# First modulation vectors by columns, squares summed on TensorE tile by tile

## What is computed

```python
m_lat = split(silu(c) @ w_mod[0] + b_mod[0], 6)          # shift, scale, gate, ...
h_lat = rmsnorm(x, g_pre_mix[0]) * (1 + m_lat[1]) + m_lat[0]
m_ctx = split(silu(c_ctx) @ w_mod[0] + b_mod[0], 6)
h_ctx = rmsnorm(ctx, g_pre_mix[0]) * (1 + m_ctx[1]) + m_ctx[0]
d = h_lat @ w_dqkv                                      # the first large product
```

## Time and profile before

| | |
|---|---|
| time of three runs | 2483.79 us median (2473.08 to 2486.47) |
| the profiled execution's own time | 2476.99 us |
| its span in the trace | 2474.6 us |
| PE busy | 2414.3 us, 98% |
| PEld busy | 1955.1 us, 79% |
| DVE busy | 1844.6 us, 75% |
| ACT busy | 1209.1 us, 49% |
| POOL busy | 612.5 us, 25% |
| granted TensorE clock, mean | 0.987 of full speed |

### The profile page before, as it was taken

The page is one execution under the profiler, slowest core; times in us unless marked ns, Lnnn a source line. Parts: engine busy times, 40 slices in busy tenths (PEclk is TensorE's granted clock), DMA queues, the critical chain, the costliest instruction groups (busy, mean ns, idle before and its releaser), DMA issues.

```text
span 2474.6 us, 32113 instructions
## 1 busy us (share of the span) xinstructions
PE 2414.3 (98%) x11124; PEld 1955.1 (79%) x11124; DVE 1844.6 (75%) x2786; ACT 1209.1 (49%) x1948; POOL 612.5 (25%) x473
## 2 busy tenths in 40 slices
PE   7989999999899999999999999999999999999998
PEld 3878888888788788888888787766887888888886
DVE  5467676767637988888655879998579888887556
ACT  3356565666643544544454542244645544445542
POOL 0058586874033300010000321100432001010002
PEclk9999998999999999999999999999999999999999
DMA  6046465652432455555865567711314555558655
GB/s 271 27 145 175 124 174 160 187 144 68 136 124 78 120 146 140 141 132 139 247 221 187 179 196 183 157 39 47 115 56 128 146 144 132 134 139 265 211 183 178
DMA packets 153203, 366.31 MB, mean 148 GB/s; under 512 B 14432, under 2 KB 15712, under 8 KB 153056
## 3 DMA queue, kind: packets, MB, share of 16 engines
q1 hardware_dynamic: 107056, 242.69, 28.4%
q0 software_dynamic: 44416, 116.93, 21.9%
q10 hardware_dynamic: 1584, 4.85, 0.6%
HBM read 303.07 MB, written 136.31 MB: 178 GB/s over the span
## 4 chain that ended last, share of the span: by engine, by line
PE 71%; DVE 18%; POOL 4%; DMA 3%; issue 3%; ACT 1%; SPq 0%; DVEq 0%; POOLq 0%; ACTq 0%
PE psum L2305 21%; PE psum L2307 21%; PE psum L2306 21%; DVE acts L2215 3%; DVE acts L2217 3%; PE psum L2521 2%; DMA set<-mod_w 1%; POOL set L837 1%; DVE weights_f32r L1850 1%; PE psum L2510 1%; PE psum L2511 1%; POOL set L836 1%; DVE acts L2219 1%; DMA low<-x_t 1%; POOL low L837 1%
## 5 line engine op out<-in xcount | busy, mean ns | idle before, releaser
L2305 PE MATMUL psum<-acts_f32r,weights_f32r 128*128 128x512 f32 x1536 | 606.4, 395 | 9.3 <-DVE acts_f32r L1610 3.0
L2307 PE MATMUL psum<-acts_f32r,weights_f32r 128*128 128x512 f32 x1536 | 599.1, 390 | 0.0
L2306 PE MATMUL psum<-acts_f32r,weights_f32r 128*128 128x512 f32 x1536 | 598.6, 390 | 0.0
L955 ACT ACTIVATE weights_f32r<-low 128x512 fp32r<-128x512 f32 (+2 forms) x471 | 303.8, 660 | 449.0 <-DVE low L1996 257.4
L2305 PEld LDWEIGHTS psum<-acts_f32r,weights_f32r 128*128 128x128 f32 x1536 | 288.9, 188 | 71.8 <-issue 6.2
L2307 PEld LDWEIGHTS psum<-acts_f32r,weights_f32r 128*128 128x128 f32 x1536 | 288.7, 188 | 61.3
L2306 PEld LDWEIGHTS psum<-acts_f32r,weights_f32r 128*128 128x128 f32 x1536 | 289.1, 188 | 58.7 <-issue 0.5
L862 POOL TENSOR_TENSOR low<-low 128x512 f32<-128x512 f32 x91 | 133.8, 1471 | 691.9 <-ACT low L1194 685.9
L2305 PE MATMUL psum<-high_f32r,weights_f32r 128*128 128x512 f32 (+1 forms) x485 | 192.1, 396 | 0.0
L2307 PE MATMUL psum<-high_f32r,weights_f32r 128*128 128x512 f32 (+1 forms) x485 | 186.9, 385 | 0.0
L2306 PE MATMUL psum<-high_f32r,weights_f32r 128*128 128x512 f32 (+1 forms) x485 | 186.8, 385 | 0.0
(11 more groups left out here) (254 smaller groups left out, 4702.0 us busy)
## 6 DMA issues: line engine op xcount, KB each, us to landing
low<-units SPq DMA_DIRECT2D x130, 512.0 KB, 4.2
set<-mod_w POOLq DMA_DIRECT2D x80, 512.0 KB, 3.9
low<-gated_sums SPq DMA_DIRECT2D x110, 256.0 KB, 4.5
low<-weight_sums SPq DMA_DIRECT2D x88, 256.0 KB, 4.1
gated_sums<-low SPq DMA_DIRECT2D x22, 768.0 KB, 3.5
low<-units SPq DMA_DIRECT2D x66, 256.0 KB, 5.0
weight_sums<-units POOLq DMA_DIRECT2D x14, 1024.0 KB, 10.1
residual<-low SPq DMA_DIRECT2D x48, 256.0 KB, 2.0
```

The source lines that it names most:

```text
L955: return act.activation(out, in_, ACT.Copy, scale=scale)
L2305: pe.matmul(out, wl, xh, start=first, stop=False, skip_group_check=continued)
L2306: pe.matmul(out, wh, xl, start=False, stop=False, skip_group_check=continued)
L2307: return pe.matmul(out, wh, xh, start=False, stop=last, skip_group_check=continued)
```

## The change

The scale and the shift vector of the first layer are made another way round. `mod_vectors` takes a 128x128 block of the weights as the stationary operand and the two columns of silu as the moving one. 8 such matmuls a tile, 64 a vector, give the result in columns at once, in bank 6 (scale) and bank 2 (shift). The copies of rows on ACT and DVE, `ROWS`, the transposes and their semaphores go.

The squares of x aren't added up on DVE any more. PE takes every squared tile as 8 stationary blocks against one column of ones, accumulating in PSUM over the tiles: 64 matmuls for 8. The squares have three buffers, and ACT waits for PE (`sq_used`) before it overwrites one. `spin` is made 16 long for 14 ahead of that, and 8 long behind the shift vector.

On PE the order becomes: scale vector, `spin`, all squares, shift tiles 0 and 1, `spread`, shift tiles 2 to 7, `spin(8, 0)`, `first_two`. On DVE the shift vector is taken up behind the sixth of the 8 `scaled`; the seventh follows it, and the eighth stands behind the third `h_low`.

```diff
-            return f(F_ACC) if n in (0, CB) else f((F_SQ if n < CB else F_LATSQ) + (n + 1) % 2 * L)
+            return f(F_SQ + n % 3 * L) if n < CB else f(F_ACC) if n == CB else f(F_LATSQ + (n + 1) % 2 * L)
...
                 square_full(k, A(k))
-                if k == 3:
-                    act.wait_ge(rows_done, 1)
-                    copy(ROWS[0:2, 0:HALF], PS[0:2, 0:HALF]).then_inc(row_out, 1)
             std(N_A, D, CB, 1)
-            act.wait_ge(rows_done, 2)
-            act.wait_ge(cols_out, 1)
-            copy(ROWS[0:2, 0:HALF], PS[0:2, 0:HALF]).then_inc(row_out, 1)
...
-            for k in range(1, CB):
-                add_square(k)
-                if k == 3:
-                    dve.wait_ge(rows_done, 1)
-                    dve.tensor_copy(ROWS[0:2, HALF:L], PS[0:2, HALF:L]).then_inc(row_out, 1)
-                if k == 5:
-                    dve.wait_ge(cols_out, 1)
-                    mod_columns(1, N_SCALE)
-                    gain(C_AV, V_PREMIX, C_MOD + CB, 1)
-                    gain(C_AX, V_PREMIX, C_MODX + CB, 1)
+            dve.wait_ge(cols_out, 1)
+            mod_columns(1, N_SCALE, 6)
+            gain(C_AV, V_PREMIX, C_MOD + CB, 1)
+            gain(C_AX, V_PREMIX, C_MODX + CB, 1)
             spread(CB, F_ACC)
             rt_here()
-            for k in range(CB):
+            for k in range(CB - 2):
                 scaled(x_block, col(C_AV), RT, k)
-            dve.wait_ge(rows_done, 2)
-            dve.tensor_copy(ROWS[0:2, HALF:L], PS[0:2, HALF:L]).then_inc(row_out, 1)
             dve.wait_ge(mod_mm, 1)
-            mod_columns(0, N_SHIFT)
+            mod_columns(0, N_SHIFT, 2)
             dve.sem_inc(shift_out, 1)
             dve.sem_inc(mod_out, 2)
+            scaled(x_block, col(C_AV), RT, CB - 2)
             for k in range(CB):
                 h_low(x_block, lambda k: h(k, 0), lambda k: h(k, 1), col(C_MOD), k)
+                if k == 2:
+                    scaled(x_block, col(C_AV), RT, CB - 1)
...
+            def mod_vectors(w, at, k, b):
+
+                for c in range(CB):
+                    mm = pe.matmul(bank(b, 2, at + 2 * c), w[:, c * P:(c + 1) * P], S[:, C_SC + 2 * k:C_SC + 2 * k + 2],
+                                   start=k == 0 and c == 0, stop=k == CB - 1 and c == CB - 1)
+                return mm
+
             spin(16, 5)
             for k in range(CB):
-
                 pe.wait_ge(scale_in[k // 2], 16)
-                for half in range(2):
-                    mm = pe.matmul(PS[0:2, half * HALF:(half + 1) * HALF], S[:, C_SC + 2 * k:C_SC + 2 * k + 2],
-                                   scale_w(k)[:, half * HALF:(half + 1) * HALF], start=k == 0, stop=k == CB - 1)
-            mm.then_inc(rows_done, 1)
-            pe.wait_ge(row_out, 2)
-            for c in range(CB):
-                mm = pe.transpose(bank(6, 2, N_SCALE + 2 * c), ROWS[0:2, c * P:(c + 1) * P], ident[0:2, 0:2])
+                mm = mod_vectors(scale_w(k), N_SCALE, k, 6)
             mm.then_inc(cols_out, 1)
-            spin(14, 5)
+            spin(16, 5)
             for k in range(CB):
-                if k == 2:
-                    pe.wait_ge(sq_used, CB - 1)
-                    col_sums(F_ACC, N_A, True, True).then_inc(sums_out, 1)
-
+                pe.wait_ge(sq_ready, k + 1)
+                for c in range(CB):
+                    mm = pe.matmul(bank(7, 1, N_A + c), sq(k)[:, c * P:(c + 1) * P], ones[:, 0:1],
+                                   start=k == 0 and c == 0, stop=k == CB - 1 and c == CB - 1)
+                mm.then_inc(sums_out if k == CB - 1 else sq_used, 1)
+            for k in range(CB):
                 pe.wait_ge(shift_in[k], 16)
-                for half in range(2):
-                    mm = pe.matmul(PS[0:2, half * HALF:(half + 1) * HALF], S[:, C_SC + 2 * k:C_SC + 2 * k + 2],
-                                   shift_w(k)[:, half * HALF:(half + 1) * HALF], start=k == 0, stop=k == CB - 1)
-                if k == 3:
+                mm = mod_vectors(shift_w(k), N_SHIFT, k, 2)
+                if k == 1:
                     spread(src=F_ACC)
-            mm.then_inc(rows_done, 1)
-            pe.wait_ge(row_out, 4)
-            for c in range(CB):
-                mm = pe.transpose(bank(6, 2, N_SHIFT + 2 * c), ROWS[0:2, c * P:(c + 1) * P], ident[0:2, 0:2])
             mm.then_inc(mod_mm, 1)
+            spin(8, 0)
```

More of the change, by code:

```diff
@@ L331, in build @@
         sums_out, std_ready, diag_ready, rt_out = sem("sums_out"), sem("std_ready"), sem("diag_ready"), sem("rt_out")
-        rows_done, row_out, cols_out = sem("rows_done"), sem("row_out"), sem("cols_out")
+        cols_out = sem("cols_out")
         ctx_sq, ctx_added, kv_sq, shift_out, h_used, kr_turned, kr_folded = (
@@ L418, in build @@
         CQ, CKV, KRT = [f(F_A + k * L) for k in range(3)], f(3072, KEYS), f(4352, KEYS)
-        ROWS = f(F_RT)
         def tap_diag(i, t):
@@ L1576, in add_square @@
             def add_square(n):
-                first = n in (1, CB + 1)
                 dve.wait_ge(sq_ready, n + 1)
-                if not first:
-                    dve.wait_ge(sq_used, n - 1 if n < CB else n - 2)
+                if n > CB + 1:
+                    dve.wait_ge(sq_used, n - 2)
                 dve.tensor_tensor(f(F_ACC), f(F_ACC), sq(n), ADD).then_inc(sq_used, 1)
@@ L1635, in ctx_block, with mod_columns @@
                 return f(F_T + k * CTX, CTX)
-            def mod_columns(vec, at):
+            def mod_columns(vec, at, b):
                 for s, dst in enumerate((C_MOD, C_MODX)):
-                    chain(mod_first(vec, dst, PS[:, 6 * HALF + at + s:6 * HALF + at + 2 * CB:2]))
+                    chain(mod_first(vec, dst, bank(b, 2 * CB, at)[:, s:2 * CB:2]))
             for u in range(2):
                 split(u)
-            for k in range(1, CB):
-                add_square(k)
-                if k == 3:
-                    dve.wait_ge(rows_done, 1)
-                    dve.tensor_copy(ROWS[0:2, HALF:L], PS[0:2, HALF:L]).then_inc(row_out, 1)
-                if k == 5:
-                    dve.wait_ge(cols_out, 1)
-                    mod_columns(1, N_SCALE)
-                    gain(C_AV, V_PREMIX, C_MOD + CB, 1)
-                    gain(C_AX, V_PREMIX, C_MODX + CB, 1)
+            dve.wait_ge(cols_out, 1)
+            mod_columns(1, N_SCALE, 6)
+            gain(C_AV, V_PREMIX, C_MOD + CB, 1)
+            gain(C_AX, V_PREMIX, C_MODX + CB, 1)
             spread(CB, F_ACC)
             rt_here()
-            for k in range(CB):
+            for k in range(CB - 2):
                 scaled(x_block, col(C_AV), RT, k)
-            dve.wait_ge(rows_done, 2)
-            dve.tensor_copy(ROWS[0:2, HALF:L], PS[0:2, HALF:L]).then_inc(row_out, 1)
             dve.wait_ge(mod_mm, 1)
-            mod_columns(0, N_SHIFT)
+            mod_columns(0, N_SHIFT, 2)
             dve.sem_inc(shift_out, 1)
             dve.sem_inc(mod_out, 2)
+            scaled(x_block, col(C_AV), RT, CB - 2)
             for k in range(CB):
                 h_low(x_block, lambda k: h(k, 0), lambda k: h(k, 1), col(C_MOD), k)
+                if k == 2:
+                    scaled(x_block, col(C_AV), RT, CB - 1)
             dve.wait_ge(ctx_sq, 1)
```

## The result

The changed kernel takes 2518.98 us (median of 4, 2512.52 to 2521.3), the kernel before 2478.43 us (median of 4). The ratio is 1.016, with a 95% interval of 1.0115 to 1.0204. The profiled execution of the changed kernel has a span of 2516.0 us.

What follows compares the result with a forecast made beforehand. PE, busy for 98% of the span, was taken as the bound, its head setting the first large product's start. A start 41.6 us later, less 1 us, gave about +40 us, put at 2519 us from a 2480 mean; range 2500 to 2531.

Steps and rivals of the forecast that it cites:

- The price of a narrow matmul: PE's fp32 matmuls of one or two moving columns: 0.112 us a record at full clock, 0.214 at the low one.
- The clock: PE's granted clock in the head: falls some 4.5 us after narrow work begins, in each stretch; bounds 2.7 and 8.
- Scale vector: First stage on PE: 23.3 us in place of 13.9, from 10.26 to 33.6.
- Squares: PE's sums of the squares of x: 128 narrow records for 16, 23.3 us, ending at 62.6.
- `spread`: PE's stage between shift tiles 1 and 2: 3.6 us at the low clock, for 1.93 at full clock.
- the term of up to 4 us in the bounds: Third narrow stretch on PE: if `spread` brings the clock back, up to 40 records are faster, -4 us.
- The shift vector: Shift tiles 2 to 7 on PE: 20.5 us, to 93.5; six `scaled` beside them, the reordering's gain swallowed.
- From the shift vector to the product: End of shift vector to first large product: 3.0 us again, but `spin(8, 0)` needs 3.4, so start at 96.9.
- The warm start: Behind the first large product's start: the clock should rise earlier with `spin` ahead, 1 us back.
- What follows: Everything behind the first large product: same durations as before, so the later start is passed on to the end.
- The rival in which the clock stays up: Head on PE: only idleness lowers the clock; product at 62.0, +4.6 us, 2482 to 2485 us; chance 11%.
- The rival that a narrow matmul costs half: PE's narrow matmuls: two columns let loads run ahead; product at 44, -11 to -13 us; chance 2%.

## Why the prediction was right

2519 us was predicted and 2518.98 measured. The mechanism was right, but that the numbers agree so closely is luck: single executions lie 5 to 10 us apart, and two errors cancelled. The start of the first large product was forecast 41.6 us later and came 39.3 later, and behind it 1 us was to be gained and 2.1 were lost, so that the span grew by 41.4 us for 40.6. The steps can be held against the trace one by one:

- **The price of a narrow matmul** held at both levels: at full clock the first 32 records of the squares took 3.50 us (0.109 each), and at the low one 96 records of the shift vector took 20.34 us (70.88 to 91.22, 0.212 each). The forecast had 0.112 and 0.214.
- **The clock** fell as said. The estimate of 4.5 us was near the 5.1 and 4.8 of the changed kernel, but other executions had 2.3 and 5.5 (order undone), 2.5 (wide squares) and 2.7 and 2.8 (squares on DVE). So this term was a range, its middle came out by chance, and the lower bound of 2.7 was a little too high.
- **Scale vector**: 33.6 was forecast, 32.6 measured. **Squares**: they were to end at 62.6 and ended at 60.5. The 2 us between the sum and the trace come from the clock holding a little longer, and from `spin` at 5.1 us for 5.7.
- **`spread`** took 3.55 us for the 3.6 estimated from the ratio of other products, and it didn't raise the clock. With the order undone the clock did come back behind it and saved 3.1 us, so the term of up to 4 us in the bounds was a real one.
- **The shift vector**: 20.3 for 20.5 us. Six `scaled` lay beside it and DVE waited 13.0 us, so the gain of the order was swallowed, as forecast; with the order undone DVE still waited 7.54 us.
- **From the shift vector to the product**: 3.4 us, of which `spin(8, 0)` at the low clock set the end, as forecast (DVE had the first low part ready some 0.2 us sooner). The start was forecast at 96.9 and came at 94.64.
- **The warm start**: the clock was low for only 2.5 us behind the start (94.64 to 97.1) for 4.4 before. 1 us was put down for it, and that is about right for this piece by itself.
- **What follows**: all of the delay was passed on; the rest of the span was 2421.4 us for 2419.3.

The rival in which the clock stays up wasn't what happened, but its sum was right: with wide operands the start was 62.17 for 62.0, and the ratio 1.0018. The rival that a narrow matmul costs half (0.056 us a record) fell with the changed kernel itself, at 0.109 with the clock at 1.00, and again with the `spin` between the narrow matmuls, where 16 records took 1.70 us.

The two parts of the loss come out nearly as worked out beforehand: weight loads and order account for 6.8 of the 39.3 us (6.7 in the forecast), the clock for 32.5 (34.9). If the clock had been left out of the sum, the forecast would have been +4.6 us, and the measured change is outside it.

## What to carry to other kernels

TensorE's busy share says nothing of the price of its work: with one or two moving columns for each 128x128 load, the long stretches here ran at half the clock for most of their length, without a gap in PE's work. Ahead of turning a product round so that the large operand becomes stationary, count the moving columns that are left, and if the weight loads set the pace anyway, repeat the moving operand until it is as wide as the load is long; here that was worth 32 us of the start and cost nothing but PSUM. Moving a step past others pays only where its engine is the late one: the same order on DVE only lengthened DVE's wait for PE in one kernel (13.03 us for 7.54), and cut a gap of PE from 3.35 to 0.96 us in the other.

## What the runs showed of the hardware

- A moving operand of 128 columns costs nearly what one of 2 columns does, at the same clock: 0.112 us a record (14.30 us for 128) for 0.106 to 0.109 (1.70 us for 16, 3.50 us for 32). Either way each record has a load of 128 columns. With 512 columns, a record of `spread` took 0.43 us at the high clock (1.71 us for 4, with wide operands throughout).
- The granted clock fell with PE busy throughout, 2.3 to 5.5 us after the narrow work began (seven falls in four executions). Once it held for 8.5 us, with the four wide records of `spread` in between. In the changed kernel it then stayed low for 54.6 us (42.5 to 97.1), through `spread`, while with the order undone it came back behind `spread` for 3.4 us.
- With the clock at its high level, 16 narrow records at a time between groups of 14 records of 128 columns kept it there for 86 us.
- The first `spin` took 5.0 to 6.5 us over the kernels, with the same instructions. Its records come slowly at first and faster later (9 in the 2.0 us from 4.70, 14 in the 1.3 us from 8.70 in the changed kernel), as in the second `spin`, in which the clock rose at 35.7 us. The profile doesn't show such a rise in the first one: its clock stands at 1.00 from the start, so in the first 9 us the pace of the records tells more than the clock shown. The length of this `spin` alone moves a head's start by 1.5 us from one execution to the next.
- Added work can be free: 36 us of `spin` between the narrow matmuls gave a ratio of 1.0173 for 1.0160, with overlapping intervals.
